# One plain iteration fewer in each of four gate stages, with part of the activation sums moved to GpSimd

## The reference

```
def swiglu_ffn(x, w_gu, w_down):                       # stages gu0 and gu1
    g, u = jnp.split(x @ w_gu, 2, axis=-1)
    return (jax.nn.silu(g) * u) @ w_down

def conv_ffn(h, w_gate, w_up, conv_w, conv_b, w_down): # stages conv0 and conv1
    g = causal_dwconv(h @ w_gate, conv_w, conv_b)
    return (jax.nn.silu(g) * (h @ w_up)) @ w_down
```

## Time and profile before

| | |
|---|---|
| median of 3 runs | 2388.21 us (2386.76 to 2393.13) |
| the profiled execution, its own time | 2386.84 us |
| its span on the core | 2385.0 us |
| PE busy | 2340.6 us, 98% of the span |
| DVE busy | 1587.9 us, 67% |
| ACT busy | 1029.4 us, 43% |
| POOL busy | 339.0 us, 14% |
| mean granted TensorE clock | 0.996 |
| gu0: first matmul, first product of seven | 247.39 us, 291.51 us |
| conv0: first matmul, first product of seven | 1446.00 us, 1515.03 us |

### The profile page before, as it was taken

The page is one execution under the profiler, slowest core; times in us unless marked ns, Lnnn a source line. Parts: engine busy times, 40 slices in busy tenths (PEclk is TensorE's granted clock), DMA queues, the critical chain, the costliest instruction groups (busy, mean ns, idle before and its releaser), DMA issues.

```text
span 2385.0 us, 36878 instructions
## 1 busy us (share of the span) xinstructions
PE 2340.6 (98%) x14899; PEld 2037.7 (85%) x14899; DVE 1587.9 (67%) x2174; ACT 1029.4 (43%) x1352; POOL 339.0 (14%) x294
## 2 busy tenths in 40 slices
PE   7699999999999999999999999999999999999999
PEld 7688899988886678999878779999888877899987
DVE  8845877846536777777585546899534545799942
ACT  6421544532225725445234444556423344455622
POOL 6402000002002240000224241000121002000000
PEclk9899999999999999999999999999999999999999
DMA  2422333233232122332333313233332212333332
GB/s 58 104 97 90 105 107 105 83 101 113 89 99 69 40 94 85 107 103 82 96 107 110 89 64 114 82 105 89 101 102 85 93 66 71 89 107 107 85 107 85
DMA packets 328844, 219.67 MB, mean 92 GB/s; under 512 B 11188, under 2 KB 319050, under 8 KB 328618
## 3 DMA queue, kind: packets, MB, share of 16 engines
q1 hardware_dynamic: 322298, 208.46, 29.6%
q0 software_dynamic: 3024, 7.90, 1.4%
q10 hardware_dynamic: 3360, 1.02, 0.2%
HBM read 206.59 MB, written 2.10 MB: 87 GB/s over the span
## 4 chain that ended last, share of the span: by engine, by line
PE 90%; DVE 4%; POOL 3%; ACT 2%; issue 1%; SPq 0%; DMA 0%; DVEq 0%; ACTq 0%; POOLq 0%
PE psum L1380 9%; PE psum L1382 9%; PE psum L1381 9%; PE psum L1136 9%; PE psum L1138 9%; PE psum L1137 9%; PE psum L1349 3%; PE psum L1350 3%; PE psum L1351 3%; PE psum L1524 2%; PE psum L1525 2%; PE psum L1526 2%; PE psum L1248 1%; PE psum L1244 1%; PE psum L1245 1%; PE psum L1228 1%
## 5 line engine op out<-in xcount | busy, mean ns | idle before, releaser
L2093 ACT CAST w_hi<-w_stage 128x2048 fp32r<-128x2048 f32 x129 | 246.7, 1912 | 691.8 <-PE psum L1138 408.4
L2973 DVE TENSOR_TENSOR w_lo<-w_stage,w_hi 128x2048 fp32r<-128x2048 f32 x126 | 300.0, 2381 | 275.6 <-ACT w_hi L2093 275.6
L1380 PE MATMUL psum<-x_sum_hi,w_hi 128*128 128x256 f32 x1088 | 308.0, 283 | 0.2 <-issue 0.2
L1382 PE MATMUL psum<-x_sum_hi,w_lo 128*128 128x256 f32 x1088 | 307.9, 283 | 0.0
L1381 PE MATMUL psum<-x_sum_lo,w_hi 128*128 128x256 f32 x1088 | 307.9, 283 | 0.0
L2163 ACT CAST w_hi<-w_parts 128x1024 fp32r<-128x1024 f32 x204 | 213.3, 1049 | 200.9 <-PE psum L1382 111.1
L3101 DVE TENSOR_TENSOR w_lo<-w_parts,w_hi 128x1024 fp32r<-128x1024 f32 x204 | 248.1, 1219 | 51.7 <-ACT w_hi L2163 50.5
L1380 PE MATMUL psum<-x_hi,w_hi 128*128 128x256 f32 x816 | 230.9, 283 | 0.0
L1381 PE MATMUL psum<-x_lo,w_hi 128*128 128x256 f32 x816 | 230.9, 283 | 0.0
L1382 PE MATMUL psum<-x_hi,w_lo 128*128 128x256 f32 x816 | 230.9, 283 | 0.0
L1136 PE MATMUL psum<-hidden_raw_hi,w_hi 128*128 128x512 f32 x572 | 223.6, 391 | 0.3 <-DVE w_lo L2973 0.3
(11 more groups left out here) (584 smaller groups left out, 5283.5 us busy)
## 6 DMA issues: line engine op xcount, KB each, us to landing
w_stage<-in_ffn_w_down_dram SPq DMA_DIRECT2D x64, 704.0 KB, 4.6
w_parts<-in_ffn_w_gu_dram SPq DMA_DIRECT2D x144, 256.0 KB, 3.4
w_parts<-in_ffn_w_gate_dram SPq DMA_DIRECT2D x64, 256.0 KB, 3.1
w_parts<-in_ffn_w_up_dram SPq DMA_DIRECT2D x64, 256.0 KB, 3.1
w_stage<-in_sb_w_qkv_dram SPq DMA_DIRECT2D x12, 1024.0 KB, 5.1
w_stage<-in_od_w_in_dram SPq DMA_DIRECT2D x12, 1024.0 KB, 5.2
w_stage<-in_ev_w_in_dram SPq DMA_DIRECT2D x10, 1024.0 KB, 5.0
w_stage<-in_ssm_w_glu_dram SPq DMA_DIRECT2D x8, 1024.0 KB, 5.5
```

The lines of the kernel that those rows point to most:

```text
L1380: nc.tensor.matmul(dst, hi, x_hi[:, k, :], start=(start and k == 0), stop=False, skip_group_check=True)
L1382: mm = nc.tensor.matmul(dst, lo, x_hi[:, k, :], start=False, stop=(k == DC // 2 - 1), skip_group_check=True)
L2093: nc.scalar.copy(whi[:, half, :], wst[:, half, :]).then_inc(whi_done, 1)
L2973: V.tensor_tensor(wlo[:, half, :], wst[:, half, :], whi[:, half, :].bitcast(F32), ALU.subtract).then_inc(wlo_done, 1)
```

## The change

The gated stages now have one plain iteration and ten of seven, the convolved ones two and nine. The work that stood between is put into the shorter lead, and part of it goes to GpSimd:

- gated stages: GpSimd makes x_sum[0] as soon as four chunks of `residual` are done, and its low part after ScalarE has rounded it (`first_block_sum`). VectorE makes the first weight sums ahead of the activation sums, then the other three sums, with the splits of x_sum[1], [2], [3] put between the splits of weights, up to those of iteration 0 of seven.
- convolved stages: GpSimd makes x_sum[2] and x_sum[3] in seven operations (`later_block_sums`), VectorE x_sum[0] and [1] in five.
- `x_bank` keeps the bank that the last iteration ends on, and the counts of the semaphores follow.

```diff
-SEVEN = {"gu0": 2, "gu1": 2, "conv0": 3, "conv1": 3}
+SEVEN = {"gu0": 1, "gu1": 1, "conv0": 2, "conv1": 2}
...
-            return bank[4 + 2 * tile + i % 2]
+            return bank[4 + 2 * tile + (SEVEN_ITERS[name] - 1 - i + (name in ("conv0", "conv1"))) % 2]
...
+            def first_block_sum(name, n):
+
+                pool.wait_ge(ln_a, affine_count(n) + DC // 2)
+                pool.wait_ge(wlo_done, (ST[name].it0 + SEVEN[name]) * 2)
+                first = [res[:, 0:DC // 2, tokens] for tokens in TOKEN_HALVES]
+                x_step(name, 1, nc.gpsimd.tensor_tensor(x_sum[0][:, :, :], first[0], first[1], ALU.subtract))
+                pool.wait_ge(rounded, rounded_count(name, 0, -4) + 1)
+                nc.gpsimd.tensor_tensor(x_sum_lo[0][:, :, :], x_sum[0][:, :, :], x_sum_hi[0][:, :, :].bitcast(F32),
+                                        ALU.subtract).then_inc(x_parts, 1)
+
+            def later_block_sums(name, n):
+
+                pool.wait_ge(x_ready, x_count(n + 1))
...
+                x_step(name, 1, nc.gpsimd.tensor_tensor(third, b22, b12, ALU.subtract))
+                x_step(name, 2, nc.gpsimd.tensor_tensor(third, third, c22, ALU.add))
+                x_step(name, 3, nc.gpsimd.tensor_tensor(third, third, c12, ALU.subtract))
+                x_step(name, 4, nc.gpsimd.tensor_tensor(fourth, third, b11, ALU.add))
+                x_step(name, 5, nc.gpsimd.tensor_tensor(fourth, fourth, c11, ALU.add))
+                x_step(name, 6, nc.gpsimd.tensor_tensor(fourth, fourth, b21, ALU.subtract))
+                x_step(name, 7, nc.gpsimd.tensor_tensor(fourth, fourth, c21, ALU.subtract))
+
             deviation_sums(0)
+            first_block_sum("gu0", 0)
             deviation_sums(1)
...
             square_sums(5)
+            later_block_sums("conv0", 5)
             square_sums(6)
...
@@ ScalarE @@
                 if conv:
-                    for n, made in ((2, 3), (3, 7), (0, 10)):
-                        round_sum(n, made)
-                    plain_gates(plain - 1, lambda: round_sum(1, 12))
+                    round_sum(2, 3, x_parts)
+                    round_sum(3, 7, x_parts)
+                    round_sum(0, 3)
+                    plain_gates(plain - 1, lambda: round_sum(1, 5))
                 else:
-                    for n, made in ((0, 1), (2, 2), (1, 3), (3, 4)):
-                        round_sum(n, made)
+                    round_sum(0, 1, x_parts)
                     plain_gates(plain - 1)
                 for n, tile in ((0, 0), (0, 1), (1, 0), (1, 1)):
+                    if not conv and (n, tile) == (1, 0):
+                        round_sum(1, 4)
                     round_pair(0, n, tile)
+                if not conv:
+                    round_sum(2, 3)
...
@@ VectorE @@
                 def start():
 
-                    plain_iteration(0)
-                    x_sums()
                     for tile in range(2):
                         sums_of_two(0, tile)
-                    for n, count in ((0, 1), (1, 3), (2, 2), (3, 4)):
-                        x_sum_low(n, count)
+                    third_and_second()
+                    low_pair(0, 0, 0)
+                    fourth()
                     for tile in range(2):
                         sum_of_three(0, tile)
-                    for tile in range(2):
-                        low_pair(0, 0, tile)
+                    plain_hidden(0, 0)
+                    low_pair(0, 0, 1)
+                    plain_hidden(0, 1)
+                    gated_low(1, 4)
                     for tile in range(2):
                         sum_of_four(0, tile)
-                    for u in range(2):
-                        plain_hidden(1, u)
                     low_pair(0, 1, 0)
 
                 def conv_start():
 
                     plain_iteration(0)
-                    x_sums_from_parts_early()
-                    plain_iteration(1)
-                    x_sums_from_parts_late()
+                    x_sums_from_parts()
                     x_sum_low(0, 3)
...
                 def iteration(i):
...
                     low_pair(i, 1, 1)
+                    if i == 0:
+                        gated_low(2, 7)
                     low_pair(i, 2, 0)
                     low_pair(i, 2, 1)
+                    if i == 0:
+                        gated_low(3, 10)
                     seed(i, 0)
```

118 lines of the change are left out of this document (75 added, 43 removed).

## The result

The changed kernel takes 2413.45 us (median of 6 runs, 2412.16 to 2417.8) against 2388.07 (6 runs beside it): a ratio of 1.0108, 95% interval 1.0098 to 1.0119. It is slower by 25.4 us, where the prediction said 12 and its range ended at 2406. The profiled execution took 2412.49 us, its span 2410.8 against 2385.0, 25.8 us more; the mean granted clock fell from 0.996 to 0.992.

What follows compares the result with a forecast made beforehand. The prediction took PE's matmuls as the bound. Two gated stages at +4.4 us (+8.8) and two convolved at +1.9 (+3.8) made +12.6 us: 2399.4 on the profiled execution, 2400.8 on the median, stated as 2400; range 2391 to 2406.

Steps and rivals of the forecast that it cites:

- One for the other saves 1.6 us per stage.: All four stages: an iteration of seven replacing a plain one saves 1.6 us of matmuls each, 6.5 us in all.
- PE starts its iterations of seven at 275.7 instead of 269.7, 6.0 us late.: Gated stages' lead: VectorE's longer queue and GpSimd's port use delay the first product; +4.4 us per stage, two +8.8.
- Less the 1.5 us of slack PE starts 2.7 us late, and `seed` ... some 0.9 more.: Convolved stages' lead: GpSimd's seven operations delay VectorE; 3.5 us late taken, +1.9 us per stage, two +3.8.
- The rest at nothing. The shifted banks of `x_bank` and the counts cost no instruction.: Remaining parts, including banks, semaphore counts, SP's loads and VectorE's work in the added iteration of seven: no cost.
- The prediction's own sign of being wrong: PE gaps ahead of the iterations of seven under 1.6 us each, or PE waiting elsewhere: w_parts loads or later iterations.
- The rival on the clock: Gated stages: PE's clock halves after the stall, losing 2.6 to 5.2 us in two stages; 2402.5 to 2405, chance 0.15.
- the two engines don't block each other: VectorE and GpSimd in the leads: no port blocking; gated stages +1.1 us each, convolved gain 1.6; 2387, chance 0.15.
- the partial rival: Either the gated norm's `x_lo` alone isn't blocked, or conv0's slack holds; 2394 to 2397 us, chance 0.15.
- the terms for late starts: Leads of all four stages, less the iteration's saving: gated +4.4 us each, convolved +1.9 each, sum +12.6.
- the forecast with the clock in two stages: The summed forecast plus half clock behind both gated stalls, 2.6 to 5.2 us: 2402.5 to 2405 us.

Runs made afterwards that it cites:

- the short filling: The change plus small matmuls on TensorE's queue ahead of the iterations of seven, 15 in gated stages, 7 in convolved: 2409.17 us, ratio 1.009.
- the run in order of deadlines: The change with, in gated stages, ring begun at slot 2, no activation sum on GpSimd, start ordered by TensorE's needs: 2396.80 us, ratio 1.0038.
- the two runs that changed the convolved stages alone: The change with GpSimd making four sum operations instead of seven there, reordered: 2409.46 us; or none, VectorE making all four sums: 2406.27 us.
- the two runs with a filling and no other edit: The change plus small matmuls ahead of the iterations of seven: 45 (gated) and 22 (convolved), 2423.69 us; 15 and 7, 2409.17 us.
- the run with the sum on VectorE: The change with no activation sum on GpSimd in gated stages, VectorE making the first sum and its low part: 2409.87 us, ratio 1.0091.

## Why the prediction was wrong

- **"One for the other saves 1.6 us per stage."** Right. Two plain iterations in the convolved stages gave 2.5 us, twice 1.6 less the 0.5 us gap, to 0.3 (the interval of that run is wider, 0 to 4 us; its trace gives the 1.1 per stage).
- **"PE starts its iterations of seven at 275.7 instead of 269.7, 6.0 us late."** Right: 275.77. That it is within 0.1 us is partly luck, since 0.3 us of the measured time lie ahead of gu0; the iteration and the lead together cost 4.1 and 3.7 us in the gated stages, forecast 4.4. The reasons stand too: `x_lo` 2.45 us, the sum on GpSimd from 258.83. Only the low part on GpSimd came behind x_sum[1] and not ahead of it.
- **"Less the 1.5 us of slack PE starts 2.7 us late, and `seed` ... some 0.9 more."** The first half is right: conv0 lead and iteration cost +1.0, which is 2.6 late less 1.6, and GpSimd's sixth operation met DVE's second plain split, which took 4.27 us against 4.4 forecast. (Its times on the way are off by some 0.3 us: 1458.9 + 5 x 2.36 + 2.2 is 1472.9 and not 1473.3.) The other 0.9 did not come in the change. Where the clock stayed up behind the same start the ninth product did wait, 0.71 us with the short filling and 0.72 in conv0 of the run in order of deadlines, but for a `w_lo` of the ring and not for `seed`; in the change the slower clock of the first products covered it.
- **"The rest at nothing. The shifted banks of `x_bank` and the counts cost no instruction."** This step failed. The counts cost no instruction, but one of them says for which product ScalarE waits, and by the ring's position it went from 12 to 14 in the gated stages and from 10 to 12 in the convolved ones. It cost 6.8 us in gaps and the clock behind one of them 2.7 more; moving the ring back in the gated stages gave 7.7. The prediction's own sign of being wrong, PE waiting elsewhere, came true here. I had looked at the start of the longer run of iterations and not at its end. What would have found it is to put the last iteration's number into every expression with a modulus.
- **The rival on the clock** came true and was held too small. I gave 2.6 us for each of the two gated stalls at a chance of 0.15, since no row of before had such a stall. In the change it came true in all four stages, at 1.5 to 1.6 us each, also behind waits of 2.4 us, and made 6.2 us; in other runs a start of a gated stage lost up to 2.7. The Trainium skill (TensorE: Matmul & The Clock Gate, why this matters for your kernels) warns of gaps over about 3 us between bursts; for the 4.32 us the trace agrees, at 2.41 us the clock fell as well (not in every run), and behind gu1's 3.10 it did not. The waits of 0.5 to 1.44 us in these runs cost nothing beyond themselves.
- **The rival "the two engines don't block each other"** is out by the 2.45 us and the 2.64 us. The sums of the partial rival are 2392.4 to 2397.2, where the text has 2394 to 2397.

Sum: the terms for late starts gave 12.6 with `seed` and measured 9.8; the clock's 8.9 (6.2 and the 2.7 of the down stage) and the ring's 6.8 were outside. The upper end of the range, 2406, is the forecast with the clock in two stages; it left no room for the clock in the convolved stages and none for the ring.

## What to carry to other kernels

A change of an iteration count moves everything that depends on the count modulo a buffer's length: work through the last iteration's slots and the waits they set, as well as the first's. Before moving an elementwise operation from VectorE to GpSimd, find the VectorE instruction with two SBUF inputs that it will meet, and add up to its whole GpSimd length there: the same operation held the port for 2.4 us on one and 1.2 on the other, and in both kinds of stage TensorE started earlier when it was undone (in the convolved ones together with a new order). And price a long TensorE wait amid dense matmuls as the wait plus a range for the clock: here waits of 2.4 to 4.3 us cost between nothing and 2.7 us beyond themselves, waits up to 1.44 us nothing.

## What the runs showed of the hardware

- The clock does not fall behind every wait of the same length. Of the waits of 3.1 to 3.2 us ahead of the two down stages, the change lost clock behind the first alone, as did the two runs that changed the convolved stages alone, the two runs with a filling and no other edit behind the second alone, the run with the sum on VectorE behind both.
- The size of the loss varies too. Behind the wait ahead of the iterations of seven in a gated stage the ten iterations took 1.5 us over their sum in the change, 2.1 and 2.2 in gu0 of those two runs, and up to 2.7 with the ring moved; two convolved stages of one execution, with the same wait of 2.4 us, lost nothing and 1.5 us. The six executions of the change alone spread over 2412.2 to 2417.8 us, and the slowest has the lowest mean clock, 0.988 against 0.992.
- What decides which wait is hit is not settled here: the versions reach it some microseconds earlier or later, and no run separates that from anything else. A single cost of this kind does not carry over from one version to the next.
- Two dependent chains, one on each of VectorE and GpSimd, take turns on the port operation by operation: 3.05, 3.31 and 3.31 us on VectorE for what takes 1.23 alone. A SCALAR_TENSOR_TENSOR with two SBUF inputs waits like a TENSOR_TENSOR (2.45 for 0.74 us). The Trainium skill (SBUF — State Buffer, two separate sides) calls the shared pair "an exclusive lock"; the rows shown here agree.
